# Two attentions of a two-block transformer: heads taken in pairs, one transposed map for differential attention, keys and values made per head for selected attention

## The chip, the cores and the metric

One core of a Trainium2 chip runs the whole program: two transformer blocks on 512 tokens of width 1024, in float32. The metric is the device time of one execution in microseconds (us), lower is better. Engines are named as in the profile: PE is the matrix engine, PEld its weight loads, DVE the vector engine, ACT the scalar engine, POOL GpSimd, SP the queue that issues most DMAs.

## What is computed

The second block's even layer has two attentions side by side. Both are touched; everything else is unchanged.

```python
def dsa_mixer(...):              # selected attention, 8 heads
    q_lat = einsum('bthd,hdc->bthc', q_nope, w_uk)          # 64 -> latent 128, per head
    qc = concatenate([q_lat, q_rope], -1)                   # 128 + 32
    kc = concatenate([c_kv, k_rope], -1)                    # one latent and one rope key for all heads
    ... the best 128 keys of each query by an index score; softmax over them ...
    o_lat = einsum('bqhk,bqkc->bqhc', p, kg[..., :128])
    o = einsum('bthc,hcd->bthd', o_lat, w_uv)               # latent 128 -> 64, per head

def diff_mixer(...):             # differential attention, 4 heads of two maps
    s = einsum('bqhmd,bshmd->bhmqs', q, k) * 64 ** -0.5
    p = safe_softmax(s, causal)
    a = p[:, :, 0] - lam_full * p[:, :, 1]
    return einsum('bhqs,bshe->bqhe', a, v)
```

## The kernel before, in words

The program is a row of stages, each a block in which every engine has its own instruction list and waits on counted semaphores; at a stage's end all engines meet. `even_mix` (L2564) runs `differential` (L2581), then `selected` (L2618), then `project_add` for the output projection.

`attention` (L805) serves both. It takes a list of units (one head, or one map of a differential head) and walks over 32 steps, one for each unit and query tile `t` of 128 queries; a step sees `128*(t+1)` keys. PE computes the scores of step s into one of three PSUM banks (L897, a second product at L899, the mask at L903 or L905), DVE takes the row maximum (L1014, and scales it at L1020 if the scale isn't 1), ACT does the exponential and its row sum (L979), DVE the reciprocal (L999) and the scaling of the whole map (L1004, with a gate L1006). Three steps later (`lag`) PE transposes the map in 128x128 pieces (L913), and ACT (odd tiles, L985) or DVE (even tiles, L953) copies it out of PSUM. Once per unit, PE multiplies values by the transposed map (`weigh`, L926: four matmuls of 512, 384, 256 and 128 columns), and ACT reads the result out (L960). PE's list is in this order by hand: score(s), transposes(s-3), and weigh at tile 1 of the next unit.

In `differential` the two maps of a head are two units; the second has the gate `minus` (minus lambda), and both accumulate in bank 7. Queries and keys have 64 rows, one map in rows 0 to 63 and one in rows 64 to 127 of the same tile.

`selected` first scores (`index_scores`), then has one stage in which three things run side by side: the projection of the `nope` queries (`project`, whose weights are split by ACT at L119 and POOL at L124), the preparation of queries against the latent keys (`up`, L2659, and `scale_up`, L2665, after the projection), and on DVE `choose`: four masked copies of the rope key (L2672, one per head of four, after a wait for three loads), and then `choose_keys` (L2811), 16 rounds of `max` and `match_replace` (L2804, L2807) and the making of `add_mask`. Then `attention` over 8 heads with two full-height products per step (L897, L899), and then a stage of its own that turns the 8 latent outputs into values (L2691) and copies them to `oT` (L2697).

`project_rope` (L557) is a projection with rotary embedding; its DVE part multiplies by a fixed `scales[b]`.

Of the kernel before, what the change touches and what calls it, by code (L numbers as in the profile page):

```python
# [18 lines left out]
ALU = mybir.AluOpType  # L19
ACT = mybir.ActivationFunctionType  # L20
AX = mybir.AxisListType

P = 128
# [473 lines left out]
def tile_of(buf, i, per_turn, b):  # L497
    return buf[:, i * per_turn + b, :]
# [58 lines left out]
def project_rope(c, w, tables, scales, dest, ahead=None, before={}, after={}):  # L557

    nc = c.nc
    per_turn = w.per_turn  # L560
    with c.stage() as ctx:
        raw = ctx.sbuf("raw", [P, per_turn, T])
        part = ctx.sbuf("part", [P, per_turn, T])
        copied, swapped, scaled = ctx.sem("copied"), ctx.sem("swapped"), ctx.sem("scaled")

        def act(eng, i, wait_tile, bank_free, split):
            for b in range(per_turn):
                wait_tile(b)
                nc.scalar.activation(raw[:, b, :], c.ps[:, b, :], ACT.Copy).then_inc(copied, 1)
                split(b)  # L570

        def pe(eng, i, b, bank_free):
            eng.wait_ge(copied, i * per_turn + (b + 1))
            nc.tensor.matmul(c.ps[:, 4 + b, :], tables[b][0][:, :], raw[:, b, :], start=True, stop=True).then_inc(swapped, 1)

        def dve(eng, i, wait_tile, bank_free):
            for b in range(per_turn):
                eng.wait_ge(swapped, i * per_turn + (b + 1))
                nc.vector.scalar_tensor_tensor(dest(i, b), c.ps[:, b, :], scales[b], tables[b][1][:, :], ALU.mult, ALU.mult).then_inc(scaled, 1)
                nc.vector.scalar_tensor_tensor(part[:, b, :], c.ps[:, 4 + b, :], scales[b], tables[b][2][:, :], ALU.mult, ALU.mult).then_inc(scaled, 1)  # L580
# [224 lines left out]
def attention(c, turns, units, scale, staging, sinks, lag=3, whole=None):  # L805
# [24 lines left out]
    with c.stage() as ctx:  # L830
# [26 lines left out]
        with nc.Block() as block:  # L857
# [135 lines left out]
            def _(dve):  # L993
# [31 lines left out]
                loop(dve, body)  # L1025

# [1554 lines left out]
def differential(c, A, w, rope64, vb, oT):  # L2581

    nc = c.nc
    with c.stage() as ctx:
# [4 lines left out]
        minus = ctx.sbuf("minus", [P, 1])  # L2589
        lam_in, dotted, exped = ctx.sem("lam_in"), ctx.sem("dotted"), ctx.sem("exped")  # L2590
# [4 lines left out]
        def minus_lambda(dve):  # L2595
            step = Chain(dve, c.dve_step)
            dve.wait_ge(lam_in, 16)
# [9 lines left out]
        project_rope(c, w["qk"], [rope64] * 4, [1.0] * 4, lambda i, b: tile_of(qkT, i, 4, b), w["iq"],  # L2607
                     {"sp": load_lambda, "dve": minus_lambda, "act": exp_lambda})

        def head_map(s, m):  # L2610
            half = slice(64 * m, 64 * m + 64)
            return dict(q=qkT[half, s, :], k=lambda i: qkT[half, s + DIFF_H, :], v=lambda j: vb[:, j, s * P:(s + 1) * P], mask=None, slots=[],
                        gate=(lambda i, t: minus[:, 0:1]) if m else None, out=c.ps[:, 7, :], sum=c.ps[:, 7, :], first=m == 0, last=m == 1)
        attention(c, 1, [head_map(s, m) for s in range(DIFF_H) for m in range(2)], 64 ** -0.5, {},
                  {2 * s + 1: (lambda i, s=s: oT[:, s + 4, :]) for s in range(DIFF_H)})


def selected(c, A, w, tables, ckv, iw, score, oT):  # L2618
# [3 lines left out]
    with c.stage() as ctx:  # L2622
        add_mask = ctx.sbuf("add_mask", [P, TT, T], BF16)
        keysT = ctx.sbuf("keysT", [P, T])
        krT = ctx.sbuf("krT", [P, 4, T])
        qrT = ctx.sbuf("qrT", [P, 2, T])
        q_lat = ctx.sbuf("q_lat", [P, DSA_H, T])
        w_uv = ctx.sbuf("w_uv", [P, DSA_H, 64])
        with c.stage() as inner:
            shared = inner.sbuf("shared", [P, 2, T])  # L2630
            w_uk = inner.sbuf("w_uk", [P, 4, P])
            head_rows = inner.sbuf("head_rows", [P, 4])
# [12 lines left out]
            qnT = inner.sbuf("qnT", [P, 4, T])  # L2645
            left.update({t: inner.sbuf(f"left{t}", [P, P * (t + 1)])[:, :] for t in range(2, TT)})
            made, copied, queries_made = inner.sem("made"), inner.sem("copied"), inner.sem("queries_made")

            def load_up(sp):
                sp.dma_start(w_uk[:, :, :], A["ev_w_uk"][0].rearrange("(j two) d c -> (two d) j c", two=2)).then_inc(up_in, 16)  # L2650
                sp.dma_start(head_rows[:, :], c.ins["c_head_rows"]).then_inc(up_in, 16)
                sp.dma_start(w_uv[:, :, :], A["ev_w_uv"][0].rearrange("h c d -> c h d")).then_inc(up_in, 16)

            def up(pe):
                pe.wait_ge(up_in, 48)
                pe.wait_ge(queries_made, 1)
                for h in range(DSA_H):
                    r = slice(64 * (h % 2), 64 * (h % 2) + 64)
                    nc.tensor.matmul(c.ps[:, h, :], w_uk[r, h // 2, :], qnT[r, h // 2, :], start=True, stop=True).then_inc(made, 1)  # L2659

            def scale_up(act):
                act.sem_inc(queries_made, 1)
                for h in range(DSA_H):
                    act.wait_ge(made, h + 1)
                    nc.scalar.activation(q_lat[:, h, :], c.ps[:, h, :], ACT.Copy, scale=A_SCALE).then_inc(copied, 1)  # L2665
                act.wait_ge(copied, DSA_H)

            def choose(dve):
# [5 lines left out]
                dve.wait_ge(masked, 4)  # L2674

            project_copy(c, w["nope"], qnT, w["out"], before={"sp": load_up, "dve": choose}, after={"pe": up, "act": scale_up})
        outT = ctx.sbuf("outT", [P, DSA_H, T])

        def head(s):
            return dict(q=q_lat[:, s, :], k=lambda i: keysT, q2=qrT[:, s // 4, :], k2=lambda i: krT[:, s % 4, :], v=lambda j: ckv[:, j, :], slots=[],  # L2680
                        mask=lambda t: add_mask[:, t, 0:P * (t + 1)], out=c.ps[:, 7, :], sum=c.ps[:, 7, :], first=True, last=True)
        attention(c, 1, [head(s) for s in range(DSA_H)], 1.0, {}, {s: (lambda i, s=s: outT[:, s, :]) for s in range(DSA_H)})
        with c.stage() as inner:
            made, copied = inner.sem("made"), inner.sem("copied")
            with nc.Block() as block:

                @block.tensor
                def _(pe):
                    for h in range(DSA_H):
                        r = slice(64 * (h % 2), 64 * (h % 2) + 64)  # L2690
                        nc.tensor.matmul(c.ps[r, h // 2, :], w_uv[:, h, :], outT[:, h, :], start=True, stop=True).then_inc(made, 1)  # L2691

                @block.scalar
                def _(act):
                    for j in range(DSA_H // 2):
                        act.wait_ge(made, 2 * j + 2)
                        nc.scalar.activation(oT[:, j, :], c.ps[:, j, :], ACT.Copy).then_inc(copied, 1)  # L2697
                    act.wait_ge(copied, DSA_H // 2)
# [383 lines left out]
def constants():  # L3082
# [9 lines left out]
        "c_head_rows": row[:, None] // 32 == np.arange(4)[None],  # L3092
# [54 lines left out]
```

## Time and profile before

| | |
|---|---|
| median of 3 runs | 3922.49 us (3922.02 to 3939.49) |
| the profiled execution | 3925.23 us, span 3923.4 us |
| granted PE clock over the span | 0.935 of full |
| differential attention | from about 2129 to 2190 us of the span |
| selected attention | from about 2356 to 2428 us |
| HBM traffic | 127 GB/s over the span |

The page of the profile gives busy times and shares for the whole span; the timeline lists instructions in order of time (start, duration, engine, line, operation, out<-in, shape, count; in square brackets the idle time before it and what ended it); the view by windows gives the busy time and the count of instructions of each engine in a stretch, in the order PE, PEld, DVE, ACT, POOL, and then the granted clock, the DMA share and GB/s. A float32 matmul has two records, one for each of its two passes.

### The profile page before, as it was taken

How to read it: one execution, taken by the hardware profiler on the slowest of the kernel's cores; microseconds unless marked ns; L12 is line 12 of the kernel's file. 1: busy time of each engine (PE TensorE's matmuls, PEld its weight loads, DVE VectorE, ACT ScalarE, POOL GpSimd, SP SyncE). 2: the span in 40 equal slices, each digit the busy share in tenths (PEclk: the TensorE clock that was granted, in tenths of full speed). 3: DMA queues.
4: the chain of work that ended last, by engine and by line, in shares of the span. 5: the costliest groups of instructions: out<-in, count | busy, mean ns of one | idle time of the engine just before them, and what ended most of it. 6: DMA issues, size and time to landing. Idle time of an engine off the chain costs nothing. (4 is left out here: it accounts for less than half of the span.)

```text
span 3923.4 us, 50300 instructions
## 1 busy us (share of the span) xinstructions
PE 3527.5 (90%) x16751; PEld 2796.5 (71%) x16755; DVE 1817.4 (46%) x3883; ACT 1317.0 (34%) x2206; POOL 1150.8 (29%) x667
## 2 busy tenths in 40 slices
PE   5979889899979999999988858999888789989988
PEld 4856676799978888888875535688766644468876
DVE  5504324877747777777744584211012155521101
ACT  3223433245533333333332324233121134433312
POOL 1312342288812222222211101244332100034432
PEclk7879999999989999999998979999998879999999
DMA  4330232245589999999822100233223300023321
GB/s 96 82 73 17 62 99 71 63 161 182 179 294 323 322 325 325 321 323 322 319 65 57 44 27 22 65 95 91 74 62 71 88 31 25 0 75 91 96 74 60
DMA packets 459491, 507.19 MB, mean 129 GB/s; under 512 B 76912, under 2 KB 401808, under 8 KB 441440
## 3 DMA queue, kind: packets, MB, share of 16 engines
q1 hardware_dynamic: 436064, 369.09, 31.0%
q0 software_dynamic: 18432, 134.23, 9.3%
q10 hardware_dynamic: 4864, 2.23, 0.3%
q8 instruction: 70, 1.15, 0.1%
q14 instruction: 61, 0.50, 0.0%
HBM read 458.07 MB, written 38.80 MB: 127 GB/s over the span
## 5 line engine op out<-in xcount | busy, mean ns | idle before, releaser
L124 POOL TENSOR_TENSOR w_low<-w_ring,w_high 128x1024 fp32r<-128x1024 f32 (+2 forms) x264 | 615.4, 2338 | 1702.6 <-ACT w_high L119 1702.6
L135 PE MATMUL ps<-h_low,w_high 128*128 128x512 f32 x1600 | 654.0, 409 | 132.1 <-POOL w_low L124 103.9
L136 PE MATMUL ps<-h_high,w_high 128*128 128x512 f32 x1600 | 641.3, 401 | 0.0
L137 PE MATMUL ps<-h_high,w_low 128*128 128x512 f32 x1600 | 639.8, 400 | 0.0
L135 PEld LDWEIGHTS ps<-h_low,w_high 128*128 128x128 f32 x1600 | 308.3, 193 | 223.9 <-POOL w_low L124 118.8
L135 PE MATMUL ps<-h_low,u_high 128*128 128x384 f32 x1024 | 352.2, 344 | 51.0 <-POOL u_low L124 41.6
L119 ACT ACTIVATE w_high<-w_ring 128x1024 fp32r<-128x1024 f32 (+2 forms) x264 | 263.3, 1012 | 299.7 <-PE ps L137 254.7
L136 PEld LDWEIGHTS ps<-h_high,w_high 128*128 128x128 f32 x1600 | 308.4, 193 | 72.5 <-issue 3.3
L137 PEld LDWEIGHTS ps<-h_high,w_low 128*128 128x128 f32 x1600 | 307.8, 192 | 72.6
L137 PE MATMUL ps<-h_high,u_low 128*128 128x384 f32 x1024 | 348.3, 340 | 0.0
L136 PE MATMUL ps<-h_high,u_high 128*128 128x384 f32 x1024 | 348.0, 340 | 0.0
L2343 POOL DMA_INDIRECT ring<-in_peer_uv_dram,idx_now x125 | 169.0, 1352 | 527.0 <-DVE sums L2479 494.3
L137 PE MATMUL ps<-v_high,weighed_low 128*128 128x512 f32 x768 | 300.4, 391 | 0.0
L136 PE MATMUL ps<-v_high,weighed_high 128*128 128x512 f32 x768 | 300.2, 391 | 0.0
L135 PE MATMUL ps<-v_low,weighed_high 128*128 128x512 f32 x768 | 298.8, 389 | 0.0
L135 PEld LDWEIGHTS ps<-h_low,u_high 128*128 128x128 f32 x1024 | 196.7, 192 | 57.9 <-POOL u_low L124 44.2
L119 ACT ACTIVATE v_high<-w_ring 128x1024 fp32r<-128x1024 f32 x128 | 135.5, 1059 | 264.7 <-PE ps L137 264.7
L521 DVE TENSOR_TENSOR xT<-xT,ps 128x512 f32 x40 | 27.5, 688 | 394.7 <-PE ps L137 394.7
L547 DVE TENSOR_TENSOR gate<-gate,ps 128x512 f32<-128x512 f32 x44 | 30.3, 689 | 387.8 <-PE ps L137 387.8
L979 ACT ACTIVATE probs<-ps,stat 128x128 f32<-128x128 f32 x224 | 118.0, 527 | 247.4 <-DVE stat L1014 211.1
L136 PEld LDWEIGHTS ps<-h_high,u_high 128*128 128x128 f32 x1024 | 196.8, 192 | 3.0
L137 PEld LDWEIGHTS ps<-h_high,u_low 128*128 128x128 f32 x1024 | 196.2, 192 | 0.0
(465 smaller groups left out, 6411.6 us busy)
## 6 DMA issues: line engine op xcount, KB each, us to landing
w_ring<-in_peer_uv_dram SPq DMA_DIRECT2D x128, 512.0 KB, 5.6
u_raw<-in_peer_uT_dram SPq DMA_DIRECT2D x80, 512.0 KB, 5.8
w_ring<-in_peer_uT_dram SPq DMA_DIRECT2D x48, 512.0 KB, 3.6
peer_gates<-ring SPq DMA_DIRECT2D x12, 2048.0 KB, 7.4
gates<-peer_gates SPq DMA_DIRECT2D x32, 768.0 KB, 10.6
w_ring<-in_ffn_w_gate_dram SPq DMA_DIRECT2D x44, 512.0 KB, 3.8
w_ring<-in_ffn_w_up_dram SPq DMA_DIRECT2D x44, 512.0 KB, 3.8
w_ring<-in_w_in_dram SPq DMA_DIRECT2D x36, 512.0 KB, 3.9
```

The lines of the kernel that those rows point to most:

```text
L119: return nc.scalar.activation(rounded(high), whole, ACT.Copy)
L124: return eng.tensor_tensor(rounded(low), whole, high, ALU.subtract)
L135: nc.tensor.matmul(out, rounded(w_high), rounded(x_low), start=start, stop=False, **more)
L136: nc.tensor.matmul(out, rounded(w_high), rounded(x_high), start=False, stop=False, **more)
L137: return nc.tensor.matmul(out, rounded(w_low), rounded(x_high), start=False, stop=stop, **more)
L521: nc.vector.tensor_tensor(d, d, c.ps[:, b, :], ALU.add).then_inc(bank_free, w.parts)
L547: nc.vector.tensor_tensor(gate[:, j, :], gate[:, j, :], c.ps[:, 2 * j + 1, :], ALU.mult).then_inc(made, 1)
L979: nc.scalar.activation(probs[:, s % p_bufs, 0:width[t]], c.ps[:, s_banks[s % len(s_banks)], 0:width[t]], ACT.Exp, bias=top[:, s % p_bufs:s ...
L2343: nc.gpsimd.indirect_dma_start(ring[:, slot, :], None, uv, bass.IndirectOffsetOnAxis(ap=index, axis=0)).then_inc(gathered[slot], 16)
```

## The change

`attention` stays for the other attentions of the program. The two attentions of the even layer use a new function, `paired_attention`, which takes two heads (or the two maps of a differential head) per step: 16 steps in place of 32 for each attention.

- Scores of both heads go to two banks, the matmuls of the two alternating (rows 0 to 63 and 64 to 127); with the next step's two, four banks in all.
- Per step DVE takes two maxima (no scaling of them any more: the factor goes into the queries, by a per-turn scalar `of_turn` in `project_rope`, or into the keys), and one reciprocal of two columns.
- The scaling of the maps moves from DVE to POOL. In differential attention POOL scales only the first map, and DVE then adds the second times (minus lambda over its sum), one instruction over the map; only this mixed map is transposed, copied and weighed. In selected attention POOL scales both maps, but for the second of the last tile, which stays on DVE.
- Selected attention has keys `knT` and values `values` per head, made from the latent before the `nope` projection in the same stage (`up`, `move_up`), so its scores are a 64-row and a 32-row product per head, and the two heads' outputs go to the two halves of bank 7. `q_lat`, the four masked copies `krT` with their constant, and the last stage (L2691, L2697) are gone. `choose_keys` is the first thing DVE does in its stage.

The diff, cut to its core:

```diff
+def paired_attention(c, pairs, lag=3):
+    n_pairs, p_bufs = len(pairs), 4
+    mixed = "mix" in pairs[0]
+    score_bank = lambda s, a: 2 * (s % 2) + a
+    pt_banks, out_bank = (4, 5, 6), 7
+    on_dve = lambda t, a: mixed and a == 1 or t == TT - 1 and a == 1
+    kinds = {t: [((0,), ("dve", "dve", "act", "act")[t])] for t in range(TT)} if mixed else {
+        0: [((0, 1), "dve")], 1: [((0, 1), "act")], 2: [((0,), "dve"), ((1,), "act")], 3: [((0,), "act"), ((1,), "dve")]}
...
+                def score(s):
+                    if s >= 2:
+                        pe.wait_ge(exped, 2 * (s - 2) + 2)
+                    for x in range(len(pair["scores"](0))):
+                        for a in range(2):
+                            q, k = pair["scores"](a)[x]
+                            nc.tensor.matmul(outs[a], q[:, t * P:(t + 1) * P], k[:, 0:w], start=x == 0, stop=False)
+                    ... mask of each head, then_inc(scored, 1)
+                def turn(s):
+                    pe.wait_ge(normed_pool, normed_by("pool", s))
+                    if normed_by("dve", s):
+                        pe.wait_ge(normed_dve, normed_by("dve", s))
+                    ... transposes of the moves of step s
+                for s in range(n_steps + lag):
+                    if s < n_steps:
+                        score(s)
+                    if s >= lag:
+                        p, t = steps[s - lag]
+                        turn(s - lag)
+                        if t == 1 and p >= 1:
+                            weigh(p - 1)
...
+            @block.gpsimd
+                        if not on_dve(t, a):
+                            pool.wait_ge(inverted, s + 1)
+                            nc.gpsimd.tensor_scalar(of, of, inverse[:, s % p_bufs, a:a + 1], None, ALU.mult).then_inc(normed_pool, 1)
...
+                def normalise(s):
+                    dve.wait_ge(exped, 2 * s + 2)
+                    v.reciprocal(inverse[:, n, :], total[:, n, :]).then_inc(summed if gated else inverted, 1)
+                    if mixed:
+                        dve.wait_ge(summed, s + 1)
+                        v.tensor_tensor(inverse[:, n, 1:2], inverse[:, n, 1:2], pair["mix"], ALU.mult).then_inc(inverted, 1)
+                        dve.wait_ge(inverted, s + 1)
+                        dve.wait_ge(normed_pool, normed_by("pool", s))
+                        v.scalar_tensor_tensor(both[0], both[1], inverse[:, n, 1:2], both[0], ALU.mult, ALU.add).then_inc(normed_dve, 1)
+                        return
+                for s in range(n_steps + lag):
+                    ... two tensor_reduce of step s, normalise(s - 1), the DVE moves of step s - lag
...
-                dve.wait_ge(up_in, 48)
-                for h in range(4):
-                    nc.vector.tensor_scalar(krT[:, h, :], shared[:, 1, :], head_rows[:, h:h + 1], None, ALU.mult).then_inc(masked, 1)
-                choose_keys(c, dve, score, best, left, add_mask)
+            def up(pe):
+                pe.wait_ge(up_in, 32)
+                ... four transposes of w_uk, one copy by ACT
+                for j in range(4):
+                    for two in range(2):
+                        r = slice(64 * two, 64 * two + 64)
+                        mm = nc.tensor.matmul(c.ps[r, banks[j], :], w_ukT[:, j, r], keysT[:, :], start=True, stop=True)
+                    mm.then_inc(made, 1)
+                for t in range(TT):
+                    pe.wait_ge(copied, t + 1)
+                    nc.tensor.matmul(c.ps[:, banks[t], :], keysT[:, t * P:(t + 1) * P], w_uv[...], start=True, stop=True).then_inc(made, 1)
+            project_copy(c, w["nope"], qnT, w["out"], before={"sp": load_up, "pe": up, "act": move_up,
+                                                              "dve": lambda dve: choose_keys(c, dve, score, best, left, add_mask)})
+            return dict(scores=lambda b: [(qnT[half(b), j, :], knT[half(b), j, :]), (qrT[rope(b), j // 2, :], shared[rope(b), 1, :])],
+                        mask=lambda t: add_mask[:, t, 0:P * (t + 1)], v=lambda b, x: values[:, x, ...64 columns], gate=None,
+                        out=lambda b: c.ps[half(b), 7, :], first=True, last=True, sink=oT[:, j, :])
+        paired_attention(c, [pair(j) for j in range(DSA_H // 2)])
-        with c.stage() as inner:      # the stage of L2691 and L2697
```

## Rows read from the trace of the kernel before

**Rows 1.** The page, part 1: busy time, share of the span and instructions.
```profile
PE 3527.5 (90%) x16751; PEld 2796.5 (71%) x16755; DVE 1817.4 (46%) x3883; ACT 1317.0 (34%) x2206; POOL 1150.8 (29%) x667
```
**Rows 2.** By windows: differential attention; the choosing stage's two halves; selected attention.
```profile
2130.00:2191.00 61.00, 58.60 (x246) 30.99 (x244) 40.22 (x144) 28.02 (x84) 0.00 (x0) 0.97 0.00 1
...
2304.00:2336.00 32.00, 27.83 (x112) 20.72 (x112) 30.60 (x62) 6.68 (x13) 7.27 (x3) 0.93 0.23 66
2336.00:2360.00 24.00, 3.66 (x10) 1.64 (x11) 17.98 (x46) 1.28 (x1) 0.00 (x0) 0.50 0.00 1
2359.00:2428.00 69.00, 67.08 (x303) 44.13 (x305) 35.19 (x112) 30.08 (x88) 0.00 (x0) 0.98 0.00 1
```
**Rows 3.** Timeline of differential attention: two reciprocals one unit apart, and a step's end.
```profile
2156.29 0.15 DVE L999 RECIPROCAL stat<-stat 128x1 f32<-128x1 f32 x1
...
2161.03 1.12 PE L897 MATMUL ps<-qkT 64*128 64x512 f32 x2
...
2162.08 0.23 PE L905 MATMUL ps<-mask_causal,mask_ident 128*128 128x128 bf16 x1
...
2163.14 0.15 DVE L999 RECIPROCAL stat<-stat 128x1 f32<-128x1 f32 x1
...
2163.33 0.42 DVE L1004 TENSOR_SCALAR probs<-probs,stat 128x384 f32<-128x384 f32 x1
...
2189.69 0.60 ACT L960 ACTIVATE oT<-ps 128x512 f32<-128x512 f32 x1 [2.51 <-PE ps L926]
```
**Rows 4.** Groups by line and shape, DVE, whole span: maxima, copies, two-input scaling.
```profile
L1014 DVE TENSOR_REDUCE stat<-ps 128x1 f32<-128x512 f32 x56 | 38.7, 691 | 37.1 <-PE ps L905 26.7 <-PE ps L903 5.4 <-DMA w_uv<-in_ev_w_uv_dram 5.0
L1014 DVE TENSOR_REDUCE stat<-ps 128x1 f32<-128x128 f32 x56 | 15.8, 282 | 36.2 <-PE ps L905 29.8 <-PE ps L903 6.4
L953 DVE COPY probsT<-ps 128x128 f32<-128x128 f32 x56 | 15.9, 283 | 0.0
L2789 DVE SCALAR_TENSOR_TENSOR vb<-relus,weights,vb 128x512 f32<-128x512 f32 x7 | 5.3, 752 | 0.3
L2789 DVE SCALAR_TENSOR_TENSOR vb<-relus,weights,vb 128x256 f32<-128x256 f32 x7 | 3.4, 484 | 0.8
```
**Rows 5.** One line's instructions on POOL: count, min/median/max ns, first and last start.
```profile
L2094 POOL TENSOR_SCALAR firsts<-keys,slots x168: 780/790/2912, 811.5 to 1078.5; 128x128 f32<-128x128 f32 x168
L124 POOL TENSOR_TENSOR w_low<-w_ring,w_high x264: 1291/2390/4730, 38.7 to 3875.6; 128x1024 fp32r<-128x1024 f32 x108, 128x896 fp32r<-128x896 f32 x16, 128x512 fp32r<-128x512 f32 x8
L124 POOL TENSOR_TENSOR w_rows_low<-w_ring,w_rows_high x11: 4502/4593/4657, 250.9 to 2938.8; 128x2048 fp32r<-128x2048 f32 x11
```
**Rows 6.** Timeline of the choosing stage.
```profile
2300.36 3.90 ACT L119 ACTIVATE w_high<-w_ring 128x1024 fp32r<-128x1024 f32 x4 [8.71 <-PEq L385]
...
2301.50 9.77 POOL L124 TENSOR_TENSOR w_low<-w_ring,w_high 128x1024 fp32r<-128x1024 f32 x4 [62.12 <-ACT w_high L119]
...
2304.75 7.20 DVE L2672 TENSOR_SCALAR krT<-shared,head_rows 128x512 f32<-128x512 f32 x4 [5.89 <-DMA w_uv<-in_ev_w_uv_dram]
...
2311.87 1.14 DVE L2804 MAX8 best<-vb 128x8 f32<-128x384 f32 x2
...
2354.28 0.19 DVE L2823 COPY add_mask<-mask_causal 128x128 bf16<-128x128 bf16 x1
```
**Rows 7.** One line's instructions on DVE, beside POOL's L124 in 657 to 732 us.
```profile
L1928 DVE MAX8 turn_top<-scores x128: 273/277/297, 657.7 to 759.4; 128x8 f32<-128x128 f32 x128
L1935 DVE MATCH_REPLACE8 scores<-turn_top,scores x64: 272/276/283, 660.1 to 758.3; 128x128 f32<-128x128 f32 x64
```
**Rows 8.** Timeline: eight matmuls with 64 rows, eight with 64 columns, and one `weigh`.
```profile
2328.95 3.70 PE L2659 MATMUL ps<-qnT,w_uk 64*128 64x512 f32 x16 [0.82 <-ACTq L2662]
...
2388.78 2.32 PE L926 MATMUL ps<-probsT,ckv 128*128 128x512 f32 x8
...
2427.01 0.60 ACT L960 ACTIVATE outT<-ps 128x512 f32<-128x512 f32 x1 [2.51 <-PE ps L926]
...
2428.46 3.65 PE L2691 MATMUL ps<-outT,w_uv 128*64 128x512 f32 x16 [1.48 <-PEq L193]
...
2432.16 0.60 ACT L2697 ACTIVATE oT<-ps 128x512 f32<-128x512 f32 x1 [0.26 <-PE ps L2691]
```
**Rows 9.** By windows: the end of the index scores, columns as in rows 2.
```profile
2275.00:2280.00 5.00, 3.73 (x7) 0.88 (x6) 4.78 (x14) 1.72 (x4) 0.00 (x0) 1.00 0.00 0
2280.00:2285.00 5.00, 4.60 (x7) 1.56 (x7) 4.71 (x13) 2.14 (x4) 0.00 (x0) 0.51 0.00 0
```

More of the change, by code:

```diff
@@ L2589, in differential @@
         minus = ctx.sbuf("minus", [P, 1])
+        of_turn = ctx.sbuf("of_turn", [P, 2])
         lam_in, dotted, exped = ctx.sem("lam_in"), ctx.sem("dotted"), ctx.sem("exped")
@@ L2596, in minus_lambda @@
             step = Chain(dve, c.dve_step)
+            step.mark(nc.vector.memset(of_turn[:, 0:1], 64 ** -0.5))
+            step.mark(nc.vector.memset(of_turn[:, 1:2], 1.0))
             dve.wait_ge(lam_in, 16)
@@ L2606, in exp_lambda, with head @@
             nc.scalar.activation(dots[:, :], dots[:, :], ACT.Exp).then_inc(exped, 1)
-        project_rope(c, w["qk"], [rope64] * 4, [1.0] * 4, lambda i, b: tile_of(qkT, i, 4, b), w["iq"],
+        project_rope(c, w["qk"], [rope64] * 4, lambda i, b: of_turn[:, bass.ds(i, 1)], lambda i, b: tile_of(qkT, i, 4, b), w["iq"],
                      {"sp": load_lambda, "dve": minus_lambda, "act": exp_lambda})
[L2610 to L2615, printed above, removed]
+        def head(s):
+            half = lambda m: slice(64 * m, 64 * m + 64)
+            return dict(scores=lambda m: [(qkT[half(m), s, :], qkT[half(m), s + DIFF_H, :])], mask=None, v=lambda m, j: vb[:, j, s * P:(s + 1) * P],
+                        mix=minus[:, 0:1], out=lambda m: c.ps[:, 7, :], first=True, last=True, sink=oT[:, s + 4, :])
+        paired_attention(c, [head(s) for s in range(DIFF_H)])
 def selected(c, A, w, tables, ckv, iw, score, oT):
@@ L2676, in selected @@
[L2676 to L2682, printed above, removed]
@@ L2683, in selected @@
-        with c.stage() as inner:
[L2684 to L2698, printed above, removed]
+                pe.wait_ge(up_in, 32)
@@ new lines, in up @@
+                for j in range(4):
+                    tr = nc.tensor.transpose(c.ps[:, 4, j * P:(j + 1) * P], w_uk[:, j, :], c.ident[:, :])
+                tr.then_inc(up_turned, 1)
+                pe.wait_ge(up_moved, 1)
+                for j in range(4):
+                    for two in range(2):
+                        r = slice(64 * two, 64 * two + 64)
+                        mm = nc.tensor.matmul(c.ps[r, banks[j], :], w_ukT[:, j, r], keysT[:, :], start=True, stop=True)
+                    mm.then_inc(made, 1)
@@ new lines, in up, with move_up @@
+                for t in range(TT):
+                    pe.wait_ge(copied, t + 1)
+                    nc.tensor.matmul(c.ps[:, banks[t], :], keysT[:, t * P:(t + 1) * P], w_uv[:, :, :].rearrange("p h d -> p (h d)"), start=True, stop=True).then_inc(made, 1)
+            def move_up(act):
+                act.wait_ge(up_turned, 1)
+                nc.scalar.activation(w_ukT[:, :, :], c.ps[:, 4, :].rearrange("p (j c) -> p j c", j=4), ACT.Copy).then_inc(up_moved, 1)
+                for j in range(4):
+                    act.wait_ge(made, j + 1)
+                    nc.scalar.activation(knT[:, j, :], c.ps[:, banks[j], :], ACT.Copy, scale=A_SCALE).then_inc(copied, 1)
+                for t in range(TT):
+                    act.wait_ge(made, 4 + t + 1)
+                    nc.scalar.activation(values[:, t, :], c.ps[:, banks[t], :], ACT.Copy).then_inc(copied, 1)
+                act.wait_ge(copied, 4 + TT)
@@ new lines, in selected, with pair @@
+            project_copy(c, w["nope"], qnT, w["out"], before={"sp": load_up, "pe": up, "act": move_up,
+                                                              "dve": lambda dve: choose_keys(c, dve, score, best, left, add_mask)})
+        def pair(j):
+            half = lambda b: slice(64 * b, 64 * b + 64)
+            rope = lambda b: slice(32 * (2 * (j % 2) + b), 32 * (2 * (j % 2) + b) + 32)
+            return dict(scores=lambda b: [(qnT[half(b), j, :], knT[half(b), j, :]), (qrT[rope(b), j // 2, :], shared[rope(b), 1, :])],
+                        mask=lambda t: add_mask[:, t, 0:P * (t + 1)], v=lambda b, x: values[:, x, (2 * j + b) * 64:(2 * j + b) * 64 + 64], gate=None,
+                        out=lambda b: c.ps[half(b), 7, :], first=True, last=True, sink=oT[:, j, :])
@@ L3090, in constants @@
         "c_keys": np.tile(np.arange(PEER_K), (P, 1)),
-        "c_head_rows": row[:, None] // 32 == np.arange(4)[None],
     }
```

154 lines of the change are left out of this document (130 added, 24 removed).

## Prediction

> **What bounds the kernel now.** I read the page's busy times first [rows 1]: PE has 90% of the span, but that is an average over stages, and the change touches three of them, some 190 us. So the second view is the one by windows [rows 2]. In both attentions PE is busy nearly all the time at almost full clock, and DVE for about half to two thirds of it. The choosing stage is different: in its second half (2336 to 2360) PE does next to nothing, the granted clock is 0.50 (the 1.2 GHz level), and DVE works through. The third view is the timeline.
>
> Selected attention is PE's own work, one piece after the other. Its 32 steps and 8 `weigh` take from 2359.3 to the last readout, which ends at 2427.6 [rows 8]: 68.3 us, 8.1 per head and 3 at the ends. A pass of 512 columns costs 0.21 us at full clock if two overlap, and 0.43 if not: eight matmuls with 64 rows (16 passes, the halves alternating) end in 3.70 us, eight with 64 columns in 3.65, where `weigh` at full height and width takes 2.32 for 8 passes of 320 columns on average, and 16 passes of 512 columns at that rate would take 7.4 [rows 8]. So two half-size matmuls do run side by side. By this unit (0.85 us for a float32 product of 512 columns, a sum of 1280 columns per head: 2.13) a head costs 2.13 + 2.13 for the two products, 0.53 for the mask, 1.07 for ten transposes and 2.13 for `weigh`: 8.0 of the 8.1.
>
> Differential attention runs at 6.85 us per unit, the distance of two reciprocals [rows 3], for 5.4 us by the same sum (one product, a short mask). The rest lies where the height of the matmul changes: the 64-row product begins at 2161.03 and has 0.85 us to do, and the mask, at full height, begins at 2162.08, 0.20 later than it could [rows 3]; the way back costs about 0.17 in the same stretch. Four such pairs make the missing 1.4 us.
>
> In the choosing stage DVE's chain of rounds is the bound: it begins at 2311.87 and its last instruction ends at 2354.5, 42.6 us later [rows 6].
>
> **Part 1, the choosing stage: 11.6 us off.** DVE stood idle for 5.89 us for the loads and then spent 7.20 us on the four masked copies [rows 6]. Both go, and the rounds can start at about 2300.3, when ACT starts [rows 6], instead of 2311.87: 11.6 us. They now run beside POOL's four L124. On another stretch the same two operations ran beside L124 with a spread of 273 to 297 and 272 to 283 ns [rows 7], so I take nothing for that; if they were slowed I would lose up to 4 us of the 11.6. What is late next: PE now does `up` ahead of the projection. Transposes and a copy 1.5 us, eight half-width matmuls 3.4 at full clock (5 with the cold start), four full ones 3.4: about 10 us, so the projection, which ended near 2328, ends near 2338. DVE's chain ends at 2343. The cover is 5 us. ACT's copies (nine of 0.6 us) delay only its fourth weight split, whose tile PE wants 15 us later; POOL's fourth L124 and SP's last `w_out` load queue behind it, needed no earlier. `q_lat` and its copies were already under DVE's chain: nothing.
>
> **Part 2, the last stage of selected attention: 5.1 us off.** From 2427.6 (end of the readout) to 2432.8 (end of the last copy) [rows 8]. The new readout writes `oT` itself.
>
> **Part 3, selected attention: 13 us off.** PE per pair of heads: 64-row products side by side 2.13; 32-row products 2.13 if they overlap too, 4.27 if not (bounds; I take the lower, since 64-row ones overlap [rows 8], and keep the other as a rival); masks 2 x 0.53; twenty transposes 2.13; `weigh` on column halves 2.13, as L2691 shows [rows 8]. That is 9.6. To it come the changes of height: three per step (64 to 32, 32 to 128, 128 to 64) at 0.17 to 0.20 [rows 3], 2.3 per pair; and about 1.0 for weight loads at the narrow tiles and the stagger of the two heads (bounds 0 and 1.5). 12.9 per pair, bounds 10.2 and 15.5. The other engines stay below: DVE has eight maxima (twice 1.95, by [rows 4]), four reciprocals, 1.7 of copies and one scaling, some 7 to 9; ACT 7 to 8; POOL seven scalings at the price worked out in part 4, 6, and 13 at its upper bound. Four pairs and 3.5 at the ends: 55 us against 68.3.
>
> Here the Trainium skill (TensorEngine Tiling, Key Properties) speaks against the change: "Mode switching requires drain", and the pair's step has three modes where the old step had one. The trace agrees for 64 against 128 rows, with its 0.20; it has no 32-row matmul beside another to show the third. Without that rule the sum would be 2.3 lower per pair, 9 us in all.
>
> **Part 4, differential attention: about 1 us on.** PE falls to 2.13 + 0.4 + 1.07 + 2.13 and switches of 1.5, with 0.3 for loads: 7.5 per head of two maps, where two units took 13.7. But DVE gets a wait: the mixing instruction waits for POOL's scaling of the same step, POOL waits for the product with lambda just before it, and behind DVE's wait stand the next step's two maxima, for which ACT waits. So POOL's time adds to DVE's. DVE per head: eight maxima 4.13 (0.28 to 0.69 us each [rows 4], plus 0.03 between), reciprocal and product 8 x 0.19 (2163.14 to 2163.33 [rows 3]), mixing at 128 to 512 columns 0.35 + 0.48 + 0.62 + 0.75 and 0.1 between (two SBUF inputs, as L2789 [rows 4]), two copies 0.7: 8.65. Handing over to POOL and back 4 x 0.25, an estimate.
>
> POOL's price is the unknown. The nearest row is L2094, 128 columns with two operations and two scalars, 780 ns [rows 5]; the slope of a two-input one is (4593 - 2390) / 1024 = 2.15 ns per column [rows 5]. Low end: half of 780 at 128 columns and half the slope, 2.4 us over the four tiles. Middle: half of 780 and the whole slope, 0.39 + 0.67 + 0.94 + 1.22 = 3.2. High end: all 780 ns go by the column, 6.1 ns each, 7.8 us. I take the middle, because a one-operation instruction should not cost more per column than one with two inputs. DVE per head 12.9, bounds 12.1 and 17.5. The Trainium skill (GPSIMD Engine Reference, Elementwise — side-by-side cycle accounting) has a one-input best case of 769 ns for 512 elements; by an estimate from it the four tiles cost at most 3.1 and the sum hardly moves. No run so far shows it.
>
> Four heads at 12.9 and 5 at the ends (the tail is longer: the last mix, transposes, copy, `weigh`, readout): 56.6. With PE streaming for under half of the time the clock may fall: in the index scores it went from 1.00 to 0.51 while matmuls came every 1.5 us and were busy for 3.73 of 5 us [rows 9]. At half clock PE's 5.8 becomes 11.5 plus switches, just DVE's time, and a long `weigh` then stalls DVE once per head. I add 2: 58.6 against 57.9 (2132.4 to 2190.3, [rows 3] for its end), about 1 us slower. `of_turn` and its two small memsets cost under 0.2 us.
>
> **Sum.** 11.6 + 5.1 + 13.3 - 1 = 29 us. The profiled execution took 3925.2, so 3896; the median of the runs is 2.7 lower, so 3894.
>
> **Rivals.**
> - *POOL's scaling goes by the column at 6.1 ns.* Differential attention 4 x 17.5 + 5 = 75, 17 slower than now; POOL also just becomes the bound of selected attention. Sum +11: 3911. For: 780 ns for 128 columns is long. Against: the slope of L124.
> - *32-row products don't run side by side.* 2.1 per pair, 8.5 us: 3902. Nothing in the trace speaks on it.
> - *Switches are hidden.* With two heads in flight the drain may be covered: selected attention at 10.4 per pair, 45; differential gains 3 with POOL at its low end. Sum +42: 3881.
> - *The choosing chain doesn't start early,* held by POOL or by PE's longer list: 8 us less, 3902.
> - *The clock falls in both loops, the slower side.* At 1.2 GHz selected attention's 9.6 of streaming doubles: 22.5 per pair, 93.5 us, 25 slower; differential at 15 per head, 65, 7 slower. With parts 1 and 2 that is +15: 3938. It turns into a loss once more than about half of the paired loops is granted at half clock. For: [rows 9]. Against: PE would be busy throughout, as in [rows 2] at 0.98.
>
> **How the numbers follow.** Forecast 0.50 (its own range 3888 to 3902), POOL by column 0.12, no overlap at 32 rows 0.13, hidden switches 0.16, chain not early 0.06, half clock 0.03. The range 3878 to 3911 leaves out the half clock and the worst of the POOL case. A measurement of this kernel can tell about 0.5% (19.6 us) from no change: below 3903 lie the forecast, the hidden switches and half of the cases at 3902: 0.75 faster. POOL by column, the other halves and the half clock at 3938 are within it: 0.23. Slower by more needs half clock and POOL together: 0.02.
>
> **What would show it.** The first MAX8 of L2804 at the stage's start beside L124, at 0.56 us for 384 columns. POOL's scaling at 0.4 to 1.2 us, and DVE's idle time in differential attention ended by POOL, not by PE. In selected attention 12.9 us from one pair's readout to the next, with gaps of 0.2 where the rows change, and both heads' products overlapping. The prediction is wrong if POOL's scaling of 512 columns takes 2 us or more, if the clock in either loop is below 0.75, or if the 32-row products come one after the other.

## Result, and the profile after

The changed kernel takes 3904.2 us (median of 7 runs, 3891.97 to 3908.07), the kernel before, run again beside it, 3932.76 (median of 7, 3922.02 to 3945.25): a ratio of 0.9922, 95% interval 0.9899 to 0.9945. The profiled executions are 3900.5 and 3925.23 us, spans 3898.5 and 3923.4, so 24.9 us lie between their spans.

First the page of the changed kernel. As in [rows 1] PE has 90% of the span; what moved is small on this scale, POOL's 48 us above all.

```profile
PE 3506.6 (90%) x16675; PEld 2771.1 (71%) x16679; DVE 1787.9 (46%) x3777; ACT 1307.5 (34%) x2187; POOL 1198.5 (31%) x711
```

The stages, read as distances in the timeline, and what the forecast had for them:

| | before | after | gained | forecast |
|---|---|---|---|---|
| differential attention, first score to end of last readout | 57.9 | 56.6 | 1.3 | -1 |
| from the end of the index scores to the first MAX8 of the choosing chain | 13.0 | 1.3 | 11.7 | 11.6 |
| selected attention, first score to end of last readout | 68.3 | 61.5 | 6.8 | 13.3 |
| from there to the first split of `oT` | 6.0 | 0.8 | 5.1 | 5.1 |

They sum to 24.9. The choosing chain, timeline of the changed kernel (start, duration, engine, line, operation, idle before):

```profile
2300.78 1.15 DVE L2985 MAX8 best<-vb 128x8 f32<-128x384 f32 x2 [1.30 <-PEq L193]
...
2302.11 9.33 POOL L124 TENSOR_TENSOR w_low<-w_ring,w_high 128x1024 fp32r<-128x1024 f32 x4 [61.96 <-ACT w_high L119]
...
2305.79 1.16 DVE L2985 MAX8 best<-left 128x8 f32<-128x384 f32 x2
...
2307.41 6.24 PE L2853 MATMUL ps<-keysT,w_ukT 128*64 128x512 f32 x16 [0.69 <-ACT w_ukT L2861]
...
2343.20 0.19 DVE L3004 COPY add_mask<-mask_causal 128x128 bf16<-128x128 bf16 x1
```

It starts with the stage and takes 42.6 us as before [rows 6], though POOL's four L124 now run beside its first 11 us. The first two MAX8 (1.15 us) are over before POOL begins; those of 2305.79 lie within POOL's 9.33 us and take 1.16, and the same third pair of the chain took 1.16 in the kernel before, when POOL was idle. PE's longer list still ended 4.3 us before DVE (2339.1 against 2343.4).

The first surprise is on POOL. Groups by shape, whole span (busy us, mean ns, idle before):

```profile
L1176 POOL TENSOR_SCALAR probs<-probs,stat 128x384 f32<-128x384 f32 x12 | 15.4, 1289 | 17.6 <-DVE stat L1187 9.1 <-DVE stat L1190 8.6
L1176 POOL TENSOR_SCALAR probs<-probs,stat 128x512 f32<-128x512 f32 x8 | 12.5, 1562 | 6.3 <-DVE stat L1190 6.3
L1176 POOL TENSOR_SCALAR probs<-probs,stat 128x256 f32<-128x256 f32 x12 | 11.0, 924 | 16.9 <-DVE stat L1187 9.9 <-DVE stat L1190 7.0
L1176 POOL TENSOR_SCALAR probs<-probs,stat 128x128 f32<-128x128 f32 x12 | 7.2, 606 | 79.8 <-DVE stat L1187 45.7 <-DVE stat L1190 34.1
```

The four tiles cost 4.4 us by these means (606, 924, 1289 and 1562 ns, which mix both attentions), where I had taken 3.2 between bounds of 2.4 and 7.8. And this time is all on DVE's path, as the waits of DVE in differential attention say (total, times, longest):

```profile
DVE probs L1194 <- POOL probs L1176: 20.6, 16, 1.8
DVE stat L1209 <- PE ps L1100: 6.2, 2, 5.8
```

16 waits for POOL, 5.15 us per head; of the two waits for PE the longest is the start of the loop. How much the clock matters meanwhile is seen by windows over two heads in turn, from one head's first exponential to the next one's:

```profile
2145.16:2157.29 12.13, 11.06 (x38) 5.42 (x38) 6.86 (x23) 5.38 (x18) 4.34 (x4) 0.57 0.01 1
2157.29:2169.42 12.13, 9.86 (x40) 4.73 (x39) 6.86 (x23) 5.87 (x20) 4.34 (x4) 0.72 0.00 0
```

The granted clock was 0.57 in the one and 0.72 in the other, and both took 12.13 us: 6.86 of DVE's work, 5.15 of waiting for POOL, and almost nothing else.

The second surprise is the clock of selected attention, by windows (columns as in [rows 2]; the granted clock stands before the last two):

```profile
2348.00:2358.00 10.00, 10.00 (x35) 3.92 (x34) 2.41 (x8) 2.74 (x11) 1.51 (x3) 0.50 0.00 0
2358.00:2368.00 10.00, 9.66 (x36) 4.83 (x36) 3.25 (x10) 3.12 (x12) 5.56 (x5) 0.50 0.01 2
2368.00:2378.00 10.00, 9.84 (x54) 4.94 (x55) 5.19 (x15) 5.21 (x19) 4.32 (x6) 0.87 0.00 1
2378.00:2388.00 10.00, 9.84 (x65) 5.14 (x62) 4.07 (x11) 4.33 (x15) 5.88 (x6) 1.00 0.01 2
```

PE is hardly ever idle (9.66 of 10 us at the least), and yet it has only 35 matmul records in the first ten microseconds and 65 in the fourth: it ran at 1.2 GHz for some 22 us from the first score (2348.2). In [rows 2] the whole stage had 0.98. Once the clock is up, the timeline of one step shows the loop as it was forecast:

```profile
2372.70 1.13 PE L1095 MATMUL ps<-knT,qnT 64*128 64x512 f32 x4
...
2373.76 1.13 PE L1095 MATMUL ps<-shared,qrT 32*128 32x512 f32 x4
...
2374.81 0.11 PEld L1098 LDWEIGHTS ps<-add_mask,mask_ident 128*128 128x128 bf16 x2 [0.76 <-issue]
...
2382.71 0.60 ACT L1148 ACTIVATE oT<-ps 128x512 f32<-128x512 f32 x1
...
2394.62 0.61 ACT L1148 ACTIVATE oT<-ps 128x512 f32<-128x512 f32 x1
```

Four records, the two passes of both heads, take the 1.13 us that two took in [rows 3] for one, and the 32-row products overlap as the 64-row ones do. From 64 rows to 32 and from 32 to 128 it is 1.05 us each, 0.85 of work and 0.20 for the change. The pair period is 11.9 us, the distance of two readouts.

### The profile page after: what moved, and what is told of

Same layout as the page of the kernel before. It is cut to its first block and busy times, and to the rows that moved or that the text cites. A ratio compares the mean times of both kernels' runs of the same rounds, so it can differ in the third digit from the quotient of the medians.

```text
span 3898.5 us, 49973 instructions
## 1 busy us (share of the span) xinstructions
PE 3506.6 (90%) x16675; PEld 2771.1 (71%) x16679; DVE 1787.9 (46%) x3777; ACT 1307.5 (34%) x2187; POOL 1198.5 (31%) x711
## 3 DMA queue, kind: packets, MB, share of 16 engines
q8 instruction: 70, 1.15, 0.1%
## 5 line engine op out<-in xcount | busy, mean ns | idle before, releaser
L124 POOL TENSOR_TENSOR w_low<-w_ring,w_high 128x1024 fp32r<-128x1024 f32 (+2 forms) x264 | 615.2, 2338 | 1511.8 <-ACT w_high L119 1511.8
L135 PE MATMUL ps<-h_low,u_high 128*128 128x384 f32 x1024 | 350.7, 342 | 52.4 <-POOL u_low L124 43.7
L135 PE MATMUL ps<-a_low,w_high 128*128 128x512 f32 x352 | 140.1, 398 | 28.9 <-POOL w_low L124 15.1
```

The source lines that it names most:

```text
L124: return eng.tensor_tensor(rounded(low), whole, high, ALU.subtract)
L135: nc.tensor.matmul(out, rounded(w_high), rounded(x_low), start=start, stop=False, **more)
```

## Experiments

The theory after the result: (1) differential attention is bound by DVE, on whose path POOL's scaling lies; (2) selected attention runs as forecast once its clock is up, and lost 9 us to the clock at its start; (3) the choosing chain is the bound of its stage. Rivals: PE at a low clock bounds differential attention too, and DVE's waits only fill the time; half-height matmuls keep the clock down whatever comes before; PE or POOL's port holds the choosing stage. Stage times below are, unless said otherwise, from the first exponential to the end of the last readout, some 1 to 2.1 us less than from the first score, as in the table; the changed kernel has 55.2 and 59.4 by this measure.

**Mixing one step later** (the wait for POOL stays, but a step later in DVE's list; the cut shows the new place, the old one in `normalise` is gone).

```diff
                     if 1 <= s <= n_steps:
                         normalise(s - 1)
+                    if mixed and 2 <= s <= n_steps + 1:
+                        mix_maps(s - 2)      # the wait for POOL and the scalar_tensor_tensor, out of normalise
```

> The changed kernel with DVE's mixing of the two maps one step later in its list, so that POOL's scaling runs beside the next step's maxima. Theory A (POOL's time stands on DVE's path: 20.6 us of DVE's idle time before the mix, 16 times): the waits before the mix go nearly to nothing, DVE's work of 8.65 us per head no longer bounds, and differential attention falls from 56.6 to 42 to 47 us. Theory B (PE at half clock is the bound, DVE's wait only fills the time): it stays at 52 us or more, and PE waits less while DVE waits for scores. Selected attention stays at 61.5 if its clock behaves as before.

Measured: differential attention 41.1 us by this measure in place of 55.2, and 42.1 from the first score in place of 56.6. The whole: 3884.6 us in one run, beside 3931.5. DVE's waits in the stage, this kernel:

```profile
DVE stat L1212 <- PE ps L1100: 9.5, 8, 5.2
DVE probs L1187 <- POOL probs L1176: 1.9, 5, 0.6
```

The 20.6 us of waiting for POOL are 1.9, 14 us came off the stage, and PE now makes DVE wait a little. POOL's scalings are as many and no faster. The granted clock of this loop was also higher, 1.00 from its start until near its end, so this run alone would leave the clock as a second reason. The two heads above speak against that: with the hop in place a head takes 12.1 us at either clock, in the changed kernel and in four more traces of its loop. So theory A holds: the hop was the bound, and the order of DVE's list makes the difference. Once the hop is gone the clock does count: in the run with both edits below the second head took 10.1 us at 0.66, where here it takes 8.1 at 1.00.

**First map scaled by DVE** in place of POOL.

```diff
+                        v.tensor_scalar(both[0], both[0], inverse[:, n, 0:1], None, ALU.mult).then_inc(normed_pool, 1)
+                        dve.wait_ge(normed_pool, s + 1)
-                        dve.wait_ge(normed_pool, normed_by("pool", s))      # and POOL's loop is empty in this attention
```

> The changed kernel with the first map scaled by DVE in place of POOL in differential attention. Per head POOL's four take 4.4 us (606, 924, 1289 and 1562 ns) and the two hand-overs about 0.5 us a step; DVE's own take 1.6 us (287 to 486 ns) and a step of 0.1 in between. Theory A: 4.4 + 2 - 2 = about 4.5 us less per head, 18 us in all, so 39 to 43 us, less what PE then holds back; I expect 42 to 46. Theory B (PE bound): 52 us or more.

Measured: 41.3 us by this measure, 42.7 from the first score, 3891.8 us in one run. DVE does more work and the stage is 14 us shorter: theory A again, from the other side. That both edits end near 41 us is no common bound. By windows over one head each, this kernel first, then the one with the late mix:

```profile
2156.55:2165.37 8.82, 7.25 (x44) 3.99 (x43) 8.40 (x27) 5.75 (x19) 0.00 (x0) 1.00 0.00 0
2148.36:2157.50 9.14, 7.47 (x44) 4.05 (x43) 7.14 (x23) 5.75 (x19) 4.97 (x5) 1.00 0.00 0
```

With the scaling on DVE, DVE is busy for 8.40 of 8.82 us: its own work is the bound. With the late mix it has 7.14 of 9.14, and 4.3 us of its waits in the stage are for PE's scores, the one at the loop's start left out.

**Twenty dummy matmuls behind the `nope` projection**, in the time in which PE waits for the choosing chain. The eight at the head of the loop stay.

```diff
             project_copy(c, w["nope"], qnT, w["out"], before={...},
+                         after={"pe": lambda pe: (pe.wait_ge(copied, 8), spin(c, 4, 20))})
```

> The changed kernel with 20 dummy matmuls after the nope projection, in the 6 us in which PE waits for DVE's choosing chain. In the changed kernel selected attention took 61.5 us (2348.2 to 2409.7), its first 20 us at a granted clock of 0.50 and then 1.00, with 11.9 us per pair there. Theory A (the shortfall against the forecast of 55 is the clock at the start): the loop starts at full clock, the stage takes 51 to 54 us, and the pair period is 11.9 from the first on. Theory B (the half-height matmuls themselves hold or bring the clock down, whatever came before): the clock falls to 0.50 again within the loop and the stage stays at 58 us or more. Differential attention is unchanged by the edit: 56.6, within 2 us.

Measured: 53.2 us by this measure (59.4 before), 54.6 from the first score. The clock of this kernel in its loop:

```profile
2349.00:2359.00 10.00, 9.85 (x60) 4.33 (x57) 4.46 (x14) 4.45 (x17) 3.60 (x5) 1.00 0.01 2
2359.00:2369.00 10.00, 9.58 (x59) 5.01 (x60) 5.45 (x15) 5.29 (x20) 6.67 (x8) 1.00 0.00 0
```

Full from the start: the twenty ran at full clock in 4.49 us, and after 1.5 us of idle time the loop's own eight did in 1.89. It stayed at 1.00 over the 48 us from 2349 to 2397, with 32- and 64-row scores in every step. Then it fell:

```profile
2397.00:2404.00 7.00, 5.77 (x24) 2.77 (x24) 0.69 (x1) 1.24 (x3) 0.00 (x0) 0.55 0.00 0
```

That cost 2.4 us in the last pair, which is why the stage took 53.2 and not the 50.8 of the runs below. Four other traces of the same loop that had reached full clock, with PE as little busy at their ends, stayed at 1.00 there; what made the difference is not shown. The whole was 3900.3 us in one run, no different from the changed kernel: differential attention began 3.8 us later there, and a single whole time can't show 6 us.

**Sixteen dummies at the head of both loops** in place of eight, PE's pause ahead of them kept.

```diff
-                spin(c, 0, 8)
+                spin(c, 0, 16)
```

> The changed kernel with 16 dummy full-height matmuls at the head of each paired loop in place of 8; the PE's idle time ahead of them stays. In the changed kernel the loop of selected attention stayed at 0.50 for 21 us after 8 of them, although PE was never idle; after dummies that ran without a pause behind the projection it was at 1.00 from the start. Theory A (full-height matmuls bring the clock up and half-height ones do not, or much later): with 8 more the clock is at 1.00 when the first score begins, and selected attention from its first exponential takes 53 us instead of 59.4, bought with 1.7 to 3.4 us of dummies. Theory B (what counts is that there was no pause): the clock is again 0.50 for some 20 us, and the stage is 2 to 3 us longer for nothing. Differential attention: within 3 us of 55.

Measured: selected attention 50.8 us, at this clock:

```profile
2351.00:2361.00 10.00, 10.00 (x60) 4.42 (x58) 4.20 (x13) 4.12 (x15) 3.34 (x5) 0.98 0.01 2
```

The 16 dummies took 6.55 us (8 took 3.57), so 8.6 us were bought with 3.0. A pause of 5.3 us before them did no harm: in these two runs the clock is up before the first 64-row matmul, and theory A holds. Differential attention took 52.9 us, but so it did behind eight dummies in the run with the heads in turn, so that is no gain of the eight more; its loop began at 1.00 and fell to 0.50 after 9 us all the same.

**Selected attention alone as changed** (`differential` as before).

> Selected attention and its choosing stage as changed, differential attention as in the kernel before. The parts by the profile of the changed kernel: choosing 11, selected attention 68.3 to 61.5, the last stage 5.1, so 23 us faster than the kernel before: a ratio near 0.994. If the parts helped each other (the clock, the memory), it would be off by more than 5 us.

Measured: 3896.5 us, ratio 0.9918 (0.9888 to 0.9948). That is more than 23 us, though the interval holds it, and the trace tells why. Its windows, differential attention (old code) first, then selected attention:

```profile
2134.00:2144.00 10.00, 10.00 (x23) 3.78 (x22) 6.08 (x23) 3.77 (x13) 0.00 (x0) 0.50 0.01 2
2144.00:2154.00 10.00, 10.00 (x31) 5.18 (x30) 4.52 (x17) 2.86 (x9) 0.00 (x0) 0.64 0.00 0
2154.00:2164.00 10.00, 10.00 (x46) 5.41 (x46) 7.60 (x28) 5.32 (x17) 0.00 (x0) 1.00 0.00 1
2355.00:2365.00 10.00, 9.69 (x57) 4.50 (x56) 4.50 (x15) 4.55 (x17) 3.77 (x5) 0.95 0.00 0
```

With eight dummies and no other help, selected attention began at nearly full clock here and took 50.8 us, 52.6 from the first score. And the old differential attention, also of 64-row scores, began at half clock and took 63.7 instead of 56.3. So the start at half clock belongs to neither version: eight dummies leave it open. Of five traces of the new selected loop behind eight dummies, four began at 0.50 (this one did not); the old differential loop began at 0.50 in two of three and stayed there for 18 us; the old selected loop, full height throughout, was at 1.00 by 4 us in each of three. The new differential loop, of paired 64-row scores, was at 1.00 by 2 us in each of eight, so half height alone does not decide it either. The profile of the kernel before happens to be one whose differential loop began at full clock, and that of the changed kernel one whose selected loop did not.

**Differential attention alone as changed** (`selected` as before).

> Differential attention as changed, selected attention and its stages as in the kernel before. By the profile of the changed kernel it takes 56.6 us against 57.9 and the rotary stage ahead of it about 0.3 more: 1 us faster, a ratio of 0.9998, no change that can be measured. A ratio below 0.997 would speak for a gain that the stage's own time does not show.

Measured: 3926.7 us, median of 10 runs, ratio 0.9997 (0.9984 to 1.001); the stage 55.1. No change, as expected, and the two parts make up the whole within their intervals (0.9918 and 0.9997 against 0.9922).

**Choosing first, in the kernel before.**

```diff
+                choose_keys(c, dve, score, best, left, add_mask)
                 dve.wait_ge(up_in, 48)
                 for h in range(4):
                     nc.vector.tensor_scalar(krT[...], shared[:, 1, :], head_rows[:, h:h + 1], None, ALU.mult).then_inc(masked, 1)
-                choose_keys(c, dve, score, best, left, add_mask)
```

> The kernel before with one reordering: choose_keys ahead of the wait for the loads and the four masked copies of the rope key. Theory A (part 1 of the forecast: the chain of rounds is the bound of its stage, and POOL's work beside it costs it nothing): the rounds start 11 us earlier, the masked copies come at the end at 0.47 us each, 1.9 in all, and selected attention starts 9 to 10 us earlier, counted from the end of the index scores. Theory B (PE's list or POOL's port holds the stage): 5 us or less. The attentions are those of the kernel before: 57.9 and 68.3 us.

Measured by the timeline, whose copies show the second effect:

```profile
2310.49 1.15 DVE L2804 MAX8 best<-vb 128x8 f32<-128x384 f32 x2 [1.32 <-PEq L193]
...
2352.92 0.19 DVE L2823 COPY add_mask<-mask_causal 128x128 bf16<-128x128 bf16 x1
...
2353.14 1.67 DVE L2673 TENSOR_SCALAR krT<-shared,head_rows 128x512 f32<-128x512 f32 x4
```

From the end of the index scores to the first exponential of selected attention 52.4 us, where it was 62.4: 10.0 off. Of part 1's 11.7 the order alone gives 10; the four copies, which took 7.20 us beside POOL [rows 6], take 1.67 with POOL idle. POOL's L124 ran beside the chain here too (2311.8 to 2321.3), and the chain took 42.6 us. Theory A. The whole time of its one run, 3922.2, does not show it: its differential attention began at half clock (63.7 us), the same toss as above.

**The heads in turn** instead of alternating.

```diff
-                    for x in range(len(pair["scores"](0))):
-                        for a in range(2):
+                    for a in range(2):
+                        for x in range(len(pair["scores"](0))):
```

> The changed kernel with both products of the first head issued before those of the second, in place of alternating. Theory A (alternating gives the overlap of the two row halves, as L2659 of the kernel before suggested): in selected attention nothing overlaps any more, streaming grows by 4.3 us per pair at full clock and there are two more changes of height per step, 1.6 per pair: the stage goes from 61.5 to about 85 us. Theory B (the array overlaps them in any order): no change. In differential attention there is one product per head, so nothing changes: 56.6.

Measured: selected attention 104.8 us by this measure (59.4), 3946.2 us in one run, slower than the kernel before. Two lines at full clock, and then its clock:

```profile
2414.02 1.12 PE L1095 MATMUL ps<-knT,qnT 64*128 64x512 f32 x2
2415.07 1.12 PE L1095 MATMUL ps<-shared,qrT 32*128 32x512 f32 x2
```
```profile
2346.00:2376.00 30.00, 30.00 (x57) 11.75 (x56) 5.14 (x16) 5.80 (x21) 7.32 (x7) 0.50 0.00 1
2376.00:2400.00 24.00, 24.00 (x52) 10.43 (x51) 5.13 (x14) 4.68 (x14) 5.46 (x6) 0.50 0.00 0
...
2404.00:2416.00 12.00, 12.00 (x42) 5.15 (x41) 3.01 (x8) 3.60 (x11) 3.00 (x4) 1.00 0.01 1
2416.00:2424.00 8.00, 8.00 (x27) 4.21 (x28) 2.73 (x8) 2.74 (x9) 4.32 (x3) 0.51 0.00 0
```

Two records now take the 1.12 us that four took: nothing overlaps, theory A. In this order neighbours in the list also differ in height, 64 and 32 rows in turn, so the run doesn't tell whether it is that or the turn of the heads that ends the overlap. I had the price at 24 us and it was 45: the clock stayed at 0.50 for 59 us from the first score (2343.1), PE busy in every one of them, went to 1.00, and at 2416 fell to 0.50 again with PE still never idle. So the loop in single file stayed at 0.50 for longer than the pairs (22 us) or the old 64-row loop with its full-height `weigh` (18 us), and it also lost the full clock once it had it. It is one trace.

**Both edits**, and a third one.

> The changed kernel with both edits: DVE's mixing one step later (it took differential attention from 56.6 to about 42.5 us) and the 20 dummies behind the nope projection (selected attention from its first exponential from 59.4 to 53.2 where it had begun at half clock). If the two places are independent: 14 us and up to 6 us on top of the changed kernel's ratio of 0.992, so a ratio to the kernel before of 0.987 to 0.989, 3878 to 3888 us. A rival: the changed kernel's loop begins at full clock in some executions anyway (it did in the run with selected attention alone), and then the dummies give nothing and the ratio is 0.988 to 0.990. Selected attention begins at 1.00 in this profile in either case.

Measured: 3879.8 us, ratio 0.9876 (0.986 to 0.9893). Differential attention 41.8, selected attention 50.8 at 1.00.

> As the run before, and in differential attention the copy of tile 1 out of PSUM moves from DVE to ACT. With the late mix a head takes 9.1 us, close to DVE's work of 8.65. Theory A (DVE is still the bound there): 0.42 us less per head, 1.5 to 2 us in all, the stage at 40 to 41. Theory B (PE or the wait for scores is the bound): no change, within 0.5 us. Neither can be told by the whole time, only by the stage.

Measured: 3875.8 us, ratio 0.9871 (0.9854 to 0.9887); the stages 41.1 and 50.8. The copy's move gave nothing (41.1 in the first late-mix run): theory B. Each of the two versions beats the changed kernel's 0.9922 with intervals that lie apart from its own; between the two there is no difference.

## Why the prediction was right, point by point

The time, 3904, lies in the range of 3878 to 3911, and the ratio, 0.9922, is close to what 3894 against 3922.5 makes (0.9927). The 10 us between 3894 and 3904 are those by which the kernel before, run again, was above the three runs that I had. But the parts did not all come as forecast: between the profiled executions 24.9 us came off for the 29 of the sum, with part 3 short by 6.5 and part 4 better by 2.3. That the errors cancelled in part was luck, and so was the side on which the clock fell: the run with selected attention alone, its loop at full clock, gained 33 us.

- **Part 1, right in size and cause.** 11.7 for 11.6; the chain unharmed beside POOL, 4.3 us of cover by PE's earlier end for my 5, and by reordering alone 10.0.
- **Part 2, right**, 5.1.
- **Part 3, right in the loop, wrong at its start.** The step that failed is "to it come ... about 1.0 for weight loads ... 12.9 per pair": the loads cost nothing, the period was 11.9, which is 9.6 of streaming and 2.3 of changes of height. At full clock the stage took 52.6 us from the first score, for 55. What I set aside with "PE would be busy throughout" was the clock: I read [rows 2] as saying that a busy PE has the full clock. In the trace of before the loop had full-height products from its first step. With its first 22 us at 0.50 the stage took 61.5. This was the mechanism of the slower rival, in one loop and at its start only: 22 us at half clock cost 9. Over the whole of both loops the granted clock was 0.75 and 0.82, at the edge of the 0.75 that I had named as a sign of being wrong.
- **The rule on mode switches** (the Trainium skill, TensorEngine Tiling, Key Properties) held for the third mode too: 0.20 us for 64 to 32 rows and for 32 to 128. The sum without it would have been 9.6 per pair, the trace has 11.9.
- **Part 4, wrong in sign, and near in size only by misses that cancel.** I had the stage 1 us slower and it was 1.3 faster. The wait for POOL stood where I had put it. POOL's scaling was mis-sized, 4.4 for 3.2 us per head, 2.5 ns per column for 2.15; with hand-overs 5.15 for 4.24 (3.2 and 1.0). The rest of DVE's time was mis-sized the other way, 7.0 for 8.65: the two maxima of a step, with nothing between them, take 1.28 us at 512 columns and not twice 0.72. 12.1 per head for 12.9. The clock did fall in this loop (0.50 to 0.72 in 2143 to 2166), but the 2 us that I had added for it were not spent while DVE was waiting: a head took 12.13 us at 0.57 and at 0.72.
- **The one-input best case of the Trainium skill** (GPSIMD Engine Reference, Elementwise — side-by-side cycle accounting), 769 ns for 512 elements: the trace has 1562 for a scaling by one scalar per row. The measurement decides; the estimate from it would have missed by a factor of two.

**Open.** What bounds the late mix at 9.1 us per head: DVE and PE each leave room there, moving a copy off DVE gave nothing, and no run took work off PE. What tips a start behind eight dummies to 0.50 or 1.00 I can't say; only the counts above stand. Nor can I say what brought the clock down within the new differential loop or at the end of the run with twenty dummies. And the share of executions of the kernel before that begin differential attention at half clock, some 7 us of its spread of 3922 to 3945, is known from three traces alone.

## What to carry to other kernels

When work moves to another engine and its result comes back within the same step, its whole time lands on the sender, however idle the receiver is (20.6 us of DVE's waiting here): put the reader one step later in its list before asking which engine is faster. Half-height matmuls overlapped here when those of the two row halves stood side by side in the list, and not when the heads came in turn; each change of height cost 0.2 us, so count the changes per step as instructions. Look at the granted clock of the first 20 us of a stage, not at its mean: a loop of part-height matmuls that began at half clock stayed there for 18 to 59 us here, and began there in six of eight traces behind eight dummies (paired differential scores left out).

## What the runs showed of the hardware

- Loops with half-height scores that began at 1.2 GHz stayed there with PE hardly ever idle: 18 us (old differential attention, two traces), 22 us (paired selected attention, three) and 59 us (heads in turn, one). At 2.4 GHz the paired selected loop stayed at 1.00 to its end in four traces that began there and fell in the last 7 us of a fifth; the loop with heads in turn fell from 1.00 to 0.50 with PE never idle. Eight dummies of full height and 512 columns (3.57 us) before the selected loop left it at either level; 16 (6.55 us) in one trace, and 20 behind the projection with 8 more at the loop in three, gave 1.00.
- A float32 scaling by one scalar per row on POOL: 606, 924, 1289 and 1562 ns for 128, 256, 384 and 512 columns.
- A two-input DVE instruction out of PSUM (L579 before, L580 after) went from 0.69 to 0.75 us when its factor became a per-row scalar in place of a number in the instruction (median of eight each, 512 columns).
- Four DVE scalings of 512 columns that took 7.20 us beside POOL took 1.67 us with POOL idle, while two MAX8 of 384 and 512 columns took 1.16 us beside POOL and without it.
